# The router's small tables: issued at the attention's end instead of behind the output weights

## What is computed

```python
merged = gt[0] * (o_a @ w_branch_a) + gt[1] * (o_g @ w_branch_g) + gt[2] * (o_m @ w_branch_m)
x1 = x + merged @ w_out
h2 = rmsnorm(x1, ffn_norm_g)
g_logit = h2 @ w_group_router + b_group_router        # 4 groups
e_logit = h2 @ w_expert_router + b_expert_router      # 32 experts, 8 per group
# top-1 group, in it top-2 experts, weights by softmax
y = x1 + sum of the chosen experts' SwiGLU (w_exp_gate, w_exp_up, w_exp_down)
```

## Time and profile before

| | |
|---|---|
| median of 3 runs | 1618.29 us (1616.92 to 1618.93) |
| profiled execution | 1617.31 us, span 1615.6 us |
| mean granted clock of TensorE | 0.966 of full speed |
| busy | PE 91%, DVE 38%, ACT 20%, POOL 7% of the span |
| weights and other data | 234.63 MB, mean 145 GB/s |
| chain that ended last | PE 77%, DMA 11%, DVE 5%, SP's queue 2% |

### The profile page before, as it was taken

How to read it: one execution, slowest core, us unless ns; L and a number is a source line. 1 busy time by engine, 2 the same in 40 slices (tenths; PEclk the granted TensorE clock), 3 DMA queues, 4 the chain that set the end, 5 groups by cost and what they waited for, 6 DMA issues and landing times.

```text
span 1615.6 us, 16891 instructions
## 1 busy us (share of the span) xinstructions
PE 1471.6 (91%) x6490; PEld 860.9 (53%) x6490; DVE 621.5 (38%) x1682; ACT 330.2 (20%) x792; POOL 113.1 (7%) x172
## 2 busy tenths in 40 slices
PE   5999999998899999987999999899998996997772
PEld 3554555445577744455677544565574454554441
DVE  2205489204564341444454444244452153111013
ACT  3214210212210001224200011334400141221210
POOL 6000000112000000001000100100000001111000
PEclk9999999999899999999999999999999997999996
DMA  7331121110422346125124240212014748999996
GB/s 212 100 113 39 40 53 26 53 52 10 148 66 78 130 156 205 57 79 209 53 65 141 80 137 1 65 27 91 27 52 123 323 157 304 420 420 419 421 418 238
DMA packets 129776, 234.63 MB, mean 145 GB/s; under 512 B 13536, under 2 KB 91360, under 8 KB 114720
## 3 DMA queue, kind: packets, MB, share of 16 engines
q1 hardware_dynamic: 116864, 186.70, 32.5%
q0 software_dynamic: 12832, 46.84, 8.0%
HBM read 215.79 MB, written 24.02 MB: 148 GB/s over the span
## 4 chain that ended last, share of the span: by engine, by line
PE 77%; DMA 11%; DVE 5%; SPq 2%; ACT 2%; issue 1%; POOL 0%; POOLq 0%; DVEq 0%; ACTq 0%
PE ps L769 18%; PE ps L661 16%; PE ps L788 7%; PE ps L717 3%; PE ps L626 3%; PE ps L1223 3%; PE ps L1289 3%; DMA arena<-in_w_exp_gate 2%; DMA bulk<-in_w_exp_down 2%; DMA bulk<-in_w_exp_gate 2%; DMA arena<-in_w_exp_up 2%; PE ps L789 2%; SPq L573 2%; PE ps L811 1%; PE ps L1312 1%; DMA arena<-in_x_sample 1%
## 5 line engine op out<-in xcount | busy, mean ns | idle before, releaser
L769 PE MATMUL ps<-bulk 128*128 128x512 f32 x688 | 302.6, 596 | 3.1 <-DVE mix L2006 1.5
L769 PEld LDWEIGHTS ps<-bulk 128*128 128x128 f32 x688 | 129.2, 191 | 157.1 <-issue 153.0
L661 PE MATMUL ps<-arena 128*128 128x320 f32 x496 | 138.2, 433 | 0.1
L788 PE MATMUL ps<-bulk 128*128 128x512 f32 x256 | 135.1, 609 | 0.0
L661 PEld LDWEIGHTS ps<-arena 128*128 128x128 f32 x496 | 94.2, 190 | 39.7 <-DVE arena L1976 0.6
L1289 PE MATMUL ps<-bulk,arena 128*64 128x256 f32 x624 | 85.0, 387 | 16.3 <-DMA bulk<-in_w_exp_up 5.8
L661 PE MATMUL ps<-arena,bulk 128*128 128x320 f32 x312 | 88.5, 432 | 0.0
L1223 PE MATMUL ps<-bulk 128*128 128x512 f32 x160 | 74.5, 621 | 10.0 <-DVE arena L2258 7.4
L789 PEld LDWEIGHTS ps<-bulk 128*128 128x128 f32 x256 | 48.6, 190 | 61.2 <-issue 61.2
L1289 PEld LDWEIGHTS ps<-bulk,arena 128*64 128x64 f32 x624 | 55.2, 140 | 43.0 <-issue 25.2
L661 PEld LDWEIGHTS ps<-arena,bulk 128*128 128x128 f32 x312 | 59.3, 190 | 24.7
(11 more groups left out here) (418 smaller groups left out, 2064.4 us busy)
## 6 DMA issues: line engine op xcount, KB each, us to landing
bulk<-in_w_in SPq DMA_DIRECT2D x48, 512.0 KB, 4.0
bulk<-in_w_exp_down SPq DMA_DIRECT2D x22, 1024.0 KB, 28.2
bulk<-in_w_exp_gate SPq DMA_DIRECT2D x20, 1024.0 KB, 29.6
bulk<-in_w_exp_up SPq DMA_DIRECT2D x19, 1024.0 KB, 24.8
bulk<-in_w_in SPq DMA_DIRECT2D x7, 2048.0 KB, 9.5
arena<-in_w_exp_up SPq DMA_DIRECT2D x13, 1024.0 KB, 29.2
arena<-in_w_exp_gate SPq DMA_DIRECT2D x12, 1024.0 KB, 22.9
arena<-in_w_exp_down SPq DMA_DIRECT2D x10, 1024.0 KB, 29.9
```

Of the source, the lines that this page charges most:

```text
L661: return [mm(dst, w[:, k, :], x[:, k, :], start=k == 0, stop=k == KH - 1) for k in range(KH)]
L769: last = mm(ps[4 + n % 2][:, :], lhs[:, k, tok:tok + P], ring[f % 2][:, k, :], start=k == 0, stop=k == KD - 1)
L788: mm(ps[b][:, 0:TP], tw[s][:, k, :], hT[:, k, 0:TP], start=k == 0, stop=k == KD - 1)
```

## The change

SP issues the six loads of the small tables inside the loop over the branch weights, ahead of the third pair (i = 2), with the same wait for the attention's end in front of them. At their old place, behind `wide_fill(12)`, they are taken out. All other waits and loads stay as they were.

```diff
--- before.py
+++ after.py
@@ -532,6 +532,15 @@
                 sp.dma_start(tw[s], w_in[:, :, c:c + P]).then_inc(tw_in[s], 16)
             wide_fill(11)
             for i in range(KH):
+                if i == 2:
+                    sp.wait_ge(oa_ok, NT * KV)
+                    sp.dma_start(gcol_e, a["ffn_norm_g"][0].rearrange("(p k) -> p k", p=P)).then_inc(rtw_in, 16)
+                    sp.dma_start(w_rt[:, :, 0:NG], a["w_group_router"][0].rearrange("(k p) g -> p k g", p=P)).then_inc(rtw_in, 16)
+                    sp.dma_start(w_rt[:, :, NG:NR], a["w_expert_router"][0].rearrange("(k p) g -> p k g", p=P)).then_inc(rtw_in, 16)
+                    with nc.allow_non_contiguous_dma(reason="one gain per partition and chunk"):
+                        sp.dma_start(gcol_f, a["ffn_norm_g"][0].rearrange("(k p) -> p k", p=P)).then_inc(rtw_in, 16)
+                    sp.dma_start(b_rt[:, 0:NG], a["b_group_router"].partition_broadcast(P)).then_inc(rtw_in, 16)
+                    sp.dma_start(b_rt[:, NG:NR], a["b_expert_router"].partition_broadcast(P)).then_inc(rtw_in, 16)
                 for q in range(2):
                     s, at = 2 * (i % 2) + q, (i + KH * q) * P
                     sp.wait_ge(t_full[s], U_MERGE[2] + 2 + i // 2)
@@ -541,14 +550,6 @@
             sp.wait_ge(xr_in, 48)
             wide_fill(12)
 
-            sp.wait_ge(oa_ok, NT * KV)
-            sp.dma_start(gcol_e, a["ffn_norm_g"][0].rearrange("(p k) -> p k", p=P)).then_inc(rtw_in, 16)
-            sp.dma_start(w_rt[:, :, 0:NG], a["w_group_router"][0].rearrange("(k p) g -> p k g", p=P)).then_inc(rtw_in, 16)
-            sp.dma_start(w_rt[:, :, NG:NR], a["w_expert_router"][0].rearrange("(k p) g -> p k g", p=P)).then_inc(rtw_in, 16)
-            with nc.allow_non_contiguous_dma(reason="one gain per partition and chunk"):
-                sp.dma_start(gcol_f, a["ffn_norm_g"][0].rearrange("(k p) -> p k", p=P)).then_inc(rtw_in, 16)
-            sp.dma_start(b_rt[:, 0:NG], a["b_group_router"].partition_broadcast(P)).then_inc(rtw_in, 16)
-            sp.dma_start(b_rt[:, NG:NR], a["b_expert_router"].partition_broadcast(P)).then_inc(rtw_in, 16)
 
 
             expert_w = (w_gate, w_up, w_down)
```

## The result

The first comparison gave 1605.53 us as the median of 7 executions, against 1616.92 for the kernel before, run beside it: a ratio of 0.9919, 95% interval 0.9895 to 0.9943. The direction and the mechanism were right, the size was taken too small: 9.8 us forecast, some 13 measured here, and 10.6 +- 0.8 once three more comparisons were in.

What follows compares the result with a forecast made beforehand. PE's progress was taken as the bound, with DVE's wait for the tables stalling it and the later weight stream following PE. Gains of 7.6 + 2.2 = 9.8 us took the median 1618.29 to 1608.5 us, range 1605.5 to 1612.5.

Steps and rivals of the forecast that it cites:

- Step 1: PE's stall at the output projection's third block, released by DVE after the tables land, goes: 7.6 us gained.
- Step 2: Slow granted clock behind the stall, in the third block, goes: 2.2 us gained, with ends at 0 and 3.9.
- Steps 3 and 5: Expert weights issued earlier, 1248.8 to about 1240.1: worth nothing; tables' small writes into SBUF under DVE's sums: at most 0.1 us.
- Step 4: Third pair's branch weights wait behind the tables on SP, issues taking 8.7 us: cost 0, covered by PE's branch products.
- A: The stall goes but the slow clock behind it stays or falls elsewhere: 1610.7 us; chance 0.14.
- B: w_out's second half lands late for the projection's sixth block, expert weights sharing the engines: 1609.8 to 1612.0 us; chance 0.06.
- C: Tables block the third pair's branch weights and PE waits; gain eaten if tables take 37.5 us; chance 0.02.
- D: No change, 1618.3 us: DVE's wait for x or a dated weight stream holds the path; 0.06, including gain lost in stream.

## Why the prediction was right and where it was off

**The bound and the path.** Right. The stall was DVE's wait for the tables, and moving that wait alone removes it. The end moved with PE: what the projection gained was still there at weight 19 and at the gather of y (360.3 us behind the projection's start in the mean of both profiles of before, 349.9 in that of the four of the changed kernel).

**Step 1, the stall.** Right in size for the profiled pair. What I had wrong is whose time it is. I treated the 7.43 us as a fixed stall and the slow stretch of 1.7 us in front of it as something that "should be missing too" or not. In fact the two are coupled. With the stall in place the third block starts 23 us behind the first whether or not the clock falls in the first two blocks: 7.43 us of stall with the slow stretch, 9.00 without it. Without the stall, PE keeps what it wins.

**Step 2, the clock.** The step that failed, as a term of the sum. I set the first stretch, the 1.7 us ahead of the stall, at zero in the likeliest case, since it stood in my one row. It came in 7 of the 12 profiles of kernels with that pause, in 1 of 2 of the kernel before and in 1 of 4 of the changed one; and by the coupling above its absence is a gain for the changed kernel alone. The third eviction shows the size. Before, it came 32.30 and 31.63 us behind the projection's start; after, 22.46, 20.88, 20.87 and 20.88. The means differ by 10.7 us, 0.9 above my 9.8. The same 10.7 stands at weight 19 (124.7 and 123.8 against 114.6, 113.4, 113.2 and 113.2), and the mean of all executions gives 10.6 +- 0.8. The part behind the stall was near: 2.2 forecast, 2.1 by the kernel with PE kept busy; but it varies as well. Against the 7.17 us of an undisturbed third block, it was 2.1 us in the first profile of before (9.23) and 1.5 in the second (8.65). The Trainium skill says that the number of slow matmuls at a start varies from run to run (TensorE: Matmul & The Clock Gate, Part 1). The traces agree for a restart behind a pause: the same 32 records took 15.64 us in one execution of before and 13.97 in the other.

**The range.** Also at fault. I took the spread of three executions, 1616.92 to 1618.93, for the scatter of a kernel. Over 85 executions the kernel before goes from 1607.95 to 1619.81 (standard deviation 2.6), the changed one over 27 from 1597.13 to 1609.94 (3.6). Worked out from the 3.6, as an estimate, a median of seven has a standard error of 1.7 us; my allowance of 1.3 was smaller than that. And the median of three that I counted from, 1618.29, was itself 2.4 us above the mean of the 85. The remainder of the first comparison's 13 us is most simply such scatter; no part of the change could be found that carries it. That is argued and not shown. That the changed kernel has a few executions below 1601 (6 of 27), while only 3 of 85 of before lie below 1610, stays unexplained; the six had a mean granted clock of 0.971 to 0.975.

**Steps 3 and 5** cost nothing, as said. With the tables at both places, or the expert weights late, the time does not move; and while the tables landed in the changed kernel, between 1168 and 1175 us, DVE's sums took 1.48 to 1.49 and 0.68 to 0.69 us each, as in the kernel before. **Step 4** cost nothing and was estimated too high, 3.9 us of issue instead of 8.7.

**Rivals.** A is excluded, the clock stays up behind the third block. B did not come: w_out's second half landed 8.0 us after its issue at 1240.75, some 20 us before its block, though ten weights of 1 MB stood behind it, and PE shows 100 records in one piece. Of C, late branch weights do cost: since 30 us of delay made a stall of 10.68, it begins at some 19 us (an estimate); the tables in the changed kernel made none, for their fills left SP when PE freed the slot. D is excluded by weight 19. Two small slips in the sums change nothing: 29.1 us from 1240.1 make 1269.2 and not 1269.4 in B, and the three chances that I added up to 0.93 make 0.92.

## What to carry to other kernels

A wait on an engine is as costly as what stands behind it in that engine's order: the scaled table was first read by PE at 1282.6 in the profile after, some 40 us behind the place of the wait, so moving the wait and moving the load were worth the same. When a stall ends at a date set by a load, slow or fast work ahead of it is hidden, so the gain from removing the stall is counted from the date and the average work, not from the idle time of one profile. And three executions are too few to say how a kernel scatters.

## What the runs showed of the hardware

- The two longest of the table issues (1024 runs of 128 bytes, 1024 of 4 bytes) held SP for 6.0 to 6.4 us together directly behind a load of 2 MB (five profiles), and for 1.2 to 2.6 us where none stood in front of them (ten profiles). The tables landed after up to 8.2 us there and up to 4.4 us otherwise.
- The granted clock fell to 1.2 GHz behind the same pause of 2.57 us in 7 of 12 profiles and stayed at 2.4 GHz in the other 5; of the two profiles of the kernel before it fell in one.
- Filling the stall with work whose result is thrown away kept the clock at 2.4 GHz and gave back some 2.1 us, with the third block still starting 22.46 us behind the first (before 23.07 and 22.98).
